# Three pieces of VectorE work moved from the levels of a triangular inverse into a chunked scan

## What is computed

```python
qkv = jax.nn.silu(causal_dwconv(jnp.concatenate([qb, kb, vb], axis=-1), conv_b[i]))
qb, kb, vb = jnp.split(qkv, [B_QK_WIDTH, 2 * B_QK_WIDTH], axis=-1)
qb = l2norm(qb...) * (DK_B ** -0.5);  kb = l2norm(kb...)
decay = jnp.exp(jnp.where(tril, g[..., :, None] - g[..., None, :], -jnp.inf))
A = jnp.eye(C) + jnp.where(strict, kkT * decay, 0.0)
sol = lax.linalg.triangular_solve(A, rhs, left_side=True, lower=True, unit_diagonal=True)
# scan over chunks: v_new = u - w @ state; o = q_exp @ state + a @ v_new; state = ...
ob = rmsnorm(ob, onorm_b[i]) * jax.nn.silu(zb)
```

## Time and profile before

| | us |
|---|---|
| median of 3 runs | 1233.89 (1231.87 to 1234.51) |
| the profiled execution | 1233.11 |
| its span | 1231.3 |
| TensorE busy | 1193.0 (97%) |
| VectorE busy | 689.6 (56%) |
| ScalarE busy | 538.4 (44%) |
| GpSimd busy | 622.6 (51%) |

### The profile page before, as it was taken

How to read it: one execution, slowest core, us unless ns; L and a number is a source line. 1 busy time by engine, 2 the same in 40 slices (tenths; PEclk the granted TensorE clock), 3 DMA queues, 4 the chain that set the end, 5 groups by cost and what they waited for, 6 DMA issues and landing times.

```text
span 1231.3 us, 19049 instructions
## 1 busy us (share of the span) xinstructions
PE 1193.0 (97%) x6526; PEld 933.2 (76%) x6526; DVE 689.6 (56%) x1157; ACT 538.4 (44%) x923; POOL 622.6 (51%) x766
## 2 busy tenths in 40 slices
PE   5989999999999999999999999999999999999998
PEld 3766776767676777766787888888888888888886
DVE  4276668685858586778340233446677723651534
ACT  4254554555454545456232212454444422432542
POOL 5643454445343453444563654466656664574552
PEclk9989999999999999999999999999999999999999
DMA  8231212221212113211222362333332342332223
GB/s 254 74 99 53 61 52 61 69 60 53 61 52 76 54 35 78 69 52 52 65 75 84 86 187 68 93 97 88 117 103 86 101 120 71 100 102 86 66 85 89
DMA packets 192404, 102.66 MB, mean 83 GB/s; under 512 B 3798, under 2 KB 191177, under 8 KB 192329
## 3 DMA queue, kind: packets, MB, share of 16 engines
q1 hardware_dynamic: 191948, 101.55, 28.9%
q10 hardware_dynamic: 381, 0.15, 0.0%
HBM read 99.57 MB, written 2.13 MB: 83 GB/s over the span
## 4 chain that ended last, share of the span: by engine, by line
PE 82%; DVE 9%; ACT 5%; issue 1%; DMA 1%; SPq 0%; DVEq 0%; ACTq 0%
PE bank L493 68%; PE bank L597 2%; PE bank L673 2%; PE bank L685 2%; PE bank L611 1%; ACT junk_k L1039 1%; PE bank L604 1%; DVE qb L1402 1%; ACT silu L976 1%; PE bank L643 1%; DVE ct L1415 1%; ACT silu L977 1%; DMA tab<-in_rel_bias 1%; DVE first_x L1439 1%; DVE oa_lo L1581 1%
## 5 line engine op out<-in xcount | busy, mean ns | idle before, releaser
L432 POOL TENSOR_TENSOR w_lo<-w_raw,w_hi 128x256 fp32r<-128x256 f32 x692 | 548.5, 826 | 259.4 <-ACT w_hi L875 253.7
L493 PE MATMUL bank<-hn_hi,w_hi 128*128 128x512 f32 x1000 | 423.6, 424 | 1.0 <-DVE o_a L1588 1.0
L493 PE MATMUL bank<-hn_hi,w_lo 128*128 128x512 f32 x1000 | 391.9, 392 | 0.0
L493 PE MATMUL bank<-hn_lo,w_hi 128*128 128x512 f32 x1000 | 391.2, 391 | 0.0
L447 POOL CAST w_hi<-w_raw 128x1024 fp32r<-128x1024 f32 x70 | 74.1, 1059 | 332.7 <-PE bank L493 319.9
L493 PEld LDWEIGHTS bank<-hn_hi,w_hi 128*128 128x128 f32 x1000 | 188.4, 188 | 49.7 <-issue 12.5
L493 PEld LDWEIGHTS bank<-hn_hi,w_lo 128*128 128x128 f32 x1000 | 188.0, 188 | 40.9
L493 PEld LDWEIGHTS bank<-hn_lo,w_hi 128*128 128x128 f32 x1000 | 188.9, 189 | 36.7 <-issue 6.5
L875 ACT ACTIVATE w_hi<-w_raw 128x1024 fp32r<-128x1024 f32 x111 | 117.9, 1062 | 76.7 <-PE bank L493 68.7
L1690 DVE SCALAR_TENSOR_TENSOR u<-vr,pt,u 128x511 f32<-128x511 f32 x88 | 89.3, 1015 | 8.0 <-DVE vr L1684 0.3
L1684 DVE TENSOR_TENSOR vr<-bank,rs 128x512 f32<-128x512 f32 x44 | 30.4, 691 | 72.3 <-PE bank L493 67.2
(11 more groups left out here) (277 smaller groups left out, 1769.8 us busy)
## 6 DMA issues: line engine op xcount, KB each, us to landing
w_raw<-in_w_in SPq DMA_DIRECT2D x73, 512.0 KB, 3.8
w_raw<-in_w_up SPq DMA_DIRECT2D x44, 512.0 KB, 3.8
w_raw<-in_w_down SPq DMA_DIRECT2D x16, 512.0 KB, 4.1
w_raw<-in_w_br_a SPq DMA_DIRECT2D x8, 512.0 KB, 4.1
w_raw<-in_w_br_b SPq DMA_DIRECT2D x8, 512.0 KB, 4.1
w_raw<-in_w_out SPq DMA_DIRECT2D x8, 512.0 KB, 4.2
w_raw<-in_w_ple_gate SPq DMA_DIRECT2D x8, 512.0 KB, 4.2
w_raw<-in_w_down SPq DMA_DIRECT2D x8, 384.0 KB, 3.4
```

Source lines behind the costliest of these rows:

```text
L432: ins = pool.tensor_tensor(wlo[c.slot][:, ks, :], raw[c.slot][:, ks, :], whi[c.slot][:, ks, :].bitcast(F32), ALU.subtract)
L493: mm = pe.matmul(acc, w[c.slot][:, i, :], xx[:, x0 + i, :], start=(i == 0 and n == 0), stop=last)
```

## The change

`finish_silu(a, 0)` leaves level 2 and `decay(a)` level 3; both go into `side`, as does `finish_ob(h - 1)` from level 6 (not in the last turn). `side` is now: the product of qb, three convolution steps of vb, `finish_ob`, `decay`. Since qb's product now comes after kb's, the values of `b_silu` swap. On ScalarE `square_q` and the exponent of `dec` leave levels 3 and 4: `square_q` follows `v_copy`, then `k_norm`, the square of oa, vb's three silu passes, z's gate and the exponent of `dec`.

```diff
@@ TensorE, k_turn
-                pe.wait_ge(sem("b_silu"), h * 2 + 2)
+                pe.wait_ge(sem("b_silu"), h * 2 + 1)
@@ ScalarE, silu_exp(h, 2) and square_q
-                    act.wait_ge(sem("b_silu"), h * 2 + 1)
+                    act.wait_ge(sem("b_silu"), h * 2 + 2)
@@ ScalarE, gate_z
-                    act.wait_ge(sem("b_silu"), (h + 1) * 2 + 2)
+                    act.wait_ge(sem("b_silu"), (h + 1) * 2 + 1)
@@ ScalarE, turn
                             done(nc.scalar.activation(eg[:, :, :], crow[:, :, :], ACT.Exp), "eg", a + 1)
-                            square_q(a)
                         if n == 4:
-                            act.wait_ge(sem("rows_read"), a + 1)
-                            done(nc.scalar.activation(dec[:, :, :], dec[:, :, :], ACT.Exp), "dec", a + 1)
                             keep_w(a, 2)
...
                     v_copy(a)
-                    silu_exp(a, 2)
+                    square_q(a)
+                    k_norm(a)
                     act.wait_ge(sem("a_out"), a + 1)
                     done(nc.scalar.activation(pr[1][:, :], bank[3][:, :], ACT.Square), "oa_sq", a + 1)
-                    k_norm(a)
+                    silu_exp(a, 2)
                     if delta and more_a:
                         gate_z(h, at("zb"), attention)
+                    act.wait_ge(sem("rows_read"), a + 1)
+                    done(nc.scalar.activation(dec[:, :, :], dec[:, :, :], ACT.Exp), "dec", a + 1)
@@ VectorE, finish_silu
-                        ("b_silu", h * 2 + (n + 1)) if n < 2 else ("vb_ready", h + 1)))
+                        ("b_silu", h * 2 + (2 - n)) if n < 2 else ("vb_ready", h + 1)))
@@ VectorE, turn
                             maxima(a, 2)
-                            steps(finish_silu(a, 0))
                     if n == 3 and attention:
-                        decay(a)
                         combine(a, 2)
...
-                    if n == 6 and h > 0:
+                    if n == 6 and h > 0 and not attention:
                         finish_ob(h - 1)
...
                 if attention:
-                    side = conv(a, 2, at("vb"))
+                    side = finish_silu(a, 0) + conv(a, 2, at("vb"))
+                    if h > 0:
+                        side = side + [lambda: finish_ob(h - 1)]
+                    side = side + [lambda: decay(a)]
```

## The result

The changed kernel takes 1226.27 us (median of six runs, 1225.86 to 1227.47) against 1233.20 us of six runs before: a ratio of 0.9945, with a 95% interval of 0.9933 to 0.9957. It is faster, by 6.9 us. The forecast was 1223.9, in a range of 1219.5 to 1228.5. The profiled execution took 1226.30 us with a span of 1224.5, so the spans differ by 6.8 us.

What follows compares the result with a forecast made beforehand. TensorE, multiplying for 97% of the span, was taken as the bound, so only its waits could be won: 6.0 + 3.7 + 0.3 = 10.0 us off 1233.11, plus 0.8 for the median, hence 1223.9; own range 1219.5 to 1226.3, 8-in-10 range to 1228.5.

Steps and rivals of the forecast that it cites:

- The levels: Seven turns with both mixers: xi 1.07 us earlier, so the 0.86 us TensorE waits at L673 vanish; 6.0 us gained.
- boundary: Chain up to ka at turn ends: oa_r 1.3 us earlier, shortening L597's wait; 0.3 us gained (0 to 0.7).
- The leading turn: Turn h = -1: combine(2) starts sooner, full clock behind L604, L567 for ka at 97.25; 3.7 us gained (0.8 to 5.0).
- reasoning on the clock: Leading turn: 2.09 us idle kept 2.4 GHz, so about 1.3 us at L604 would too; 6.0 us become 3.0.
- rival of the clock: Leading turn: clock falls anyway, there or before L567; some 3 us return, gain there 0.8, time 1226.8; chance 0.17.
- The scan: VectorE's moved work in the scan: product fills a hole, decay differences take 1.14 us; cost 0, hidden by fill.
- rival of decay under GpSimd: Scan: differences as slow as in the leading turn beside GpSimd; 1.2 us lost in seven turns, 8.4 us, 1232.3; chance 0.09.
- The queue: SP's weight loads: crow and loads behind it leave later, yet land in time for GpSimd and TensorE; cost 0.
- mild form of decay's rival: Scan: decay slowed under GpSimd at a mostly partial price; of the case's 0.09 chance, 0.07 counted as faster.

Runs made afterwards that it cites:

- product only: Kernel before with only qb's product and square_q moved into the scan; decay differences, finish_ob and ScalarE's other order as before: 1230.82 us, ratio 0.9983.
- product with ScalarE's order: Changed kernel with decay differences, finish_ob and dec's exponent put back in the levels; qb's product, square_q and k_norm's order stay changed: 1222.19 us, ratio 0.9913.
- ScalarE's order only: Kernel before with only k_norm and oa's square put ahead of vb's silu on ScalarE; VectorE untouched: 1232.30 us, ratio 0.9992.
- decay with the product: Changed kernel with the four decay differences right behind qb's product, both in the scan's first slot: 1223.43 us, ratio 0.9918.
- leading turn only: The whole change in the leading turn only; turns 0 to 6 keep the order of the kernel before: 1230.54 us, ratio 0.9983.
- cast held: Changed kernel with only GpSimd edited: in turns 1 to 4 its cast waits until the decay differences are done: 1224.20 us, ratio 0.9923.
- decay first: Changed kernel with decay and finish_ob swapped in side, so decay stands ahead of the state of t=2: 1222.40 us, ratio 0.9916.
- decay only: Kernel before with only the decay differences and dec's exponent moved, the differences to the changed kernel's slot: 1235.90 us, ratio 1.0021.
- last version: Changed kernel with decay ahead of finish_ob, dec's exponent behind ka's square in the leading turn, four oa_lo pieces in the last: 1221.39 us, ratio 0.9900.
- second profile of before: Kernel before, unedited, profiled once more: 1232.19 us; its leading turn ended at 103.16.

## Why the prediction was right, and where it wasn't

**The levels, 6.0 us: right**, and slightly small. Every L673 of turns 0 to 6 runs without a wait, and the stretch is 0.92 us shorter, 6.4 in all. What the step did not say is that this gain is only kept with ScalarE's new order: product only loses it all at ka. The prediction used that order in its boundary term and gave it 0.3 us; in fact it carries the 6.4: product only and product with ScalarE's order differ in nothing else, and their turns take 67.1 and 65.75 us.

**The leading turn, 3.7 us: right against this profile, in part by luck.** 3.5 us are the change's own, and the two marks on the way agree: L567 at 97.05 (97.25 forecast), its wait 2.24 (2.5). L604 came at 74.35 (74.65). But the 3.5 contains the long fall of that one execution of before; against the second it is 2.4. The text moved both pieces for it, where the product alone was enough. The reasoning on the clock was wrong as a rule. It had 2.09 us of idleness keep 2.4 GHz and 3.16 lose it. ScalarE's order only shows the reverse with the same two waits, and behind 2.23 or 2.24 at L567 the clock fell in three profiles (decay with the product, leading turn only, cast held) and did not in five (the change twice, decay first, decay only, product only). In the last version it fell behind 2.09 us as well. The Trainium skill (TensorE: Matmul & The Clock Gate, What's actually happening) calls the number of matmuls run at the lower clock at a kernel's start run-variable; no reading here bears on a kernel's start. For pauses within a kernel the runs show waits equal to 0.02 us with and without a fall, but in kernels that differ elsewhere; the two kernels profiled twice gave the same outcome twice, and only the length of the fall differed. So the 3.0 us was one execution's value (the second profile of before ran 3.4 us at half clock, (1 - 0.57) x 2 x 4.00, not 6.0), and the rival of the clock is not excluded but priced: 1.0 to 1.2 us behind L567, and not 3.

**The boundary, 0.3 us: about 0.5.** Decay first shortens turns 1 to 3 by 1.00, the level by 0.92, so 0.1 comes from a turn's end, in six turns. ScalarE's order alone gave 0.12 to 0.14 there.

**The scan, 0: the step that failed.** The text had decay last 1.14 "without disturbance" and wrote that with VectorE 0.3 us slower the cover would be gone. It took 1.34 us longer in turns 1 to 4 and cost 0.87 in each: 3.5 us. The rival of decay under GpSimd had the mechanism, at 8.4 us in seven turns and a chance of 0.09. It also had the place in four of them: the cast lies over decay's second half. In the other three it doesn't: in turn 0 there is no `finish_ob` and decay stands one slot earlier, in turn 5 the cast waits for its load, in turn 6 it comes later (551.63, with decay over at 550.34). What was off is the price by which the text held it against the rival: it scaled the leading turn's 3.29 us by the half that would lie under the cast, 1.7 in all, and found that near the limit; it was 2.48. The runs show a block instead: the third difference lasts from 216.88 to 218.01, as long as the cast does, and with `finish_ob` in place of decay the cast is the one that waits. The Trainium skill (SBUF — State Buffer, SBUF: two separate sides) has this rule: where a VectorE instruction has two SBUF inputs and GpSimd's instruction reads SBUF, the pair of ports that they share is held for a whole instruction by the one that starts first. The trace agrees on both sides, 1.13 us for a difference of 0.35 and 1.59 for a cast of 1.04. It isn't exact: the second difference (216.61 to 216.96) overlaps the cast's start (216.80), and neither is longer for it. The leading turn of before had the form already, had its four differences been read one by one: 0.81 to 1.01 us each, beside a cast and subtractions of 0.73. The fourth difference (0.91) pays once more, beside the subtraction.

**The queue, 0: nearly right.** The loads leave where it said (418.67 for crow in turn 4 and 483.91 in turn 5; the forecast's 424 and 491 are counted in before's times, in which these turns start 5.3 and 5.6 us later, so turn 5's is 1.5 sooner than forecast) and no product of TensorE waits for weights. The margin was read from TensorE alone; the late split, 7.9 us later in the turn where 6 were forecast, costs 0.4 us in turn 5 by another way, ka's product beside its cast. It is shown as far as crow 1.1 us sooner in the turn goes with 0.75 instead of 1.54 for that product, and as far as the cast held, which leaves turn 5 as it is, keeps its 66.14; the split alone wasn't moved.

**The sum.** 6.4 in the levels, 3.5 in the leading turn and 0.5 at the boundaries, less 3.5 in the scan and 0.4 in turn 5, is 6.5. The changed kernel's profile also reached the leading turn 0.4 us sooner, which makes 6.9; the spans give 6.8. The time came out in the stated range although a loss of 3.5 us had stood at 0 in the forecast: 1226.27 is at the edge of the forecast's own range (to 1226.3), and inside the wider one because that one made room for the clock and for a mild form of decay's rival.

## What to carry to other kernels

Work that is moved off a critical place must be priced by who runs beside it at its new place, in that kernel's own schedule: here four operations of 0.35 us were free in one slot and cost 0.87 us a turn when they started 1.1 us later (50.95 instead of 49.84 us into turn 4). Where VectorE works beside GpSimd as here, count a whole instruction of the other engine as the possible delay (1.13 us for 0.35 in these traces), and keep a consumer that TensorE waits for from standing right behind such work. And before a gain is credited to the move, try the parts alone: the product's move won nothing in the full turns without ScalarE's order, and decay's move won nothing anywhere: in the full turns it was free in the best slots and cost 0.87 us in the change's, and in the leading turn it cost 0.6 us.

## What had not been expected of the hardware

The clock of TensorE fell behind waits of 2.1 to 2.2 us in some executions and held through waits of 3.16 in one, in kernels that differ elsewhere and whose waits are the same to 0.1 us. In the leading-turn-only kernel the ten times lie in two groups, 1230.06 to 1230.68 (six) and 1231.46 to 1232.12 (four); that they are runs without and with the fall is likely from its price of 1.2 us and from the profiled one (1231.62, with the fall), but only that one was profiled. A single profile's clock should not be put into a sum as a certain term.
